# Two-branch attention layer: order of input-projection panels changed, sums of weights formed on VectorE

## Chip, cores and metric

One core of a Trainium2 chip runs the kernel. The metric is the device time of one execution in microseconds.

## The reference

One decoder layer on x of 1024 tokens x 2048 channels, all in float32, with a conditioning vector c of 2048:

```
shift, scale, gate = split(c @ w_ada + b_ada, 3)            # each 2048
h    = layer_norm(x) * (1 + scale) + shift
proj = h @ w_in       # 3 x 1024 (fox q,k,v), 8 forget logits, 1024 + 256 + 256 (swa q,k,v),
                      # 1024 + 1024 (g_fox, g_swa), 2048 + 2048 (m_fox, m_swa)
o_fox = forgetting_attention(8 heads of 128, causal, bias = differences of cumsum(log_sigmoid(logits)))
o_swa = sliding_window_attention(16 query heads of 64, 4 key/value heads, window 128, ALiBi, sinks)
y_fox = (o_fox * silu(g_fox)) @ w_br_fox ;  y_swa = (o_swa * silu(g_swa)) @ w_br_swa
merged = sigmoid(m_fox) * y_fox + sigmoid(m_swa) * y_swa
out  = layer_norm(2**0.25 * x + gate * (merged @ w_out)) * ln_g + ln_b
```

## The kernel before

Each engine has its own instruction stream, written out by hand, and they meet at semaphores. DMAs are issued by SyncE (SP), and some by GpSimd and ScalarE.

**Prologue.** Eight row blocks of x (128 x 2048) are loaded into a ring of four, their statistics taken (x_stat, x_scale on VectorE, x_norm on ScalarE) and transposed on TensorE. The part of shift and scale that the first half of the channels needs (c @ w_ada) is formed in four rounds: ada_sum on VectorE for half of the weights, ada_multiply on TensorE for the other half, ada_turn, ada_take. Loads for a round go out when its slots of the previous round are used.

**Input projection.** The output has 84 blocks of 128 channels (queries, keys and values of both branches: 36; gates g: 16; m: 32), and is formed transposed, as channels x tokens. The inner dimension is split into two panels of 1024. A group is two blocks in one panel, and is formed by a scheme of Strassen's kind with seven products in place of eight: `dense(q, lo, hi)` issues matmuls lo to hi of group q, `product(q, k)` being 12 of them (4 slices x 3 float32r parts: high x high, high x low, low x high), each 128x128 by 128x512. The factors on the weights' side are three blocks of the weights themselves and four sums or differences of blocks (`weight_sums`, on GpSimd at L580, into w_sum). Each factor is rounded to its high part on ScalarE (`weight_high`, L726) and its low part is formed on VectorE (`weight_low`, L1049). The factors of the activations' side, b_hi and b_lo, stay in SBUF for all groups of a panel. Weights of group q + 1 are loaded (`load_in`, L414, 1024 KB) once the last low part of group q that reads w_raw is formed. Products go through the PSUM banks pC, pA, pD, pC, pA, pC, pA; ScalarE takes the first use of a tile of ctile (`take`, L740), VectorE adds the others (`join`, L1056). After product k both engines do a fixed list of work in `after(q, k)`, waiting for the product first; ScalarE's list for k = 2 has the high part of the first factor of group q + 1, so it waits there for the load.

**Order.** GROUPS is 42. Groups 0 to 41 are panel one of all blocks; their results are stored to proj_scratch by SP (L433). Then panel two's operands replace panel one's in b_hi and b_lo (`renew`), and groups 42 to 83 are panel two, added to proj_scratch by DMAs with accumulation that GpSimd issues (L624): 10 groups (PRE) alone, 16 beside local attention, one in each unit (Q_SWA on), 16 beside forgetting attention, two in each head (Q_FOX on). FOX_AT tells after how many matmuls of a head's groups each row block's transposes stand, FOX_AFTER which steps `after` come in the row block.

**Conditioning of the rest.** The other half of shift and scale, and gate, are formed in four parts on VectorE, two bg_steps (L1081) in each of groups 0 to 31, from 2 x 512 KB a group that SP loads. Then bg_sum on TensorE adds over partitions.

**Attention.** A local unit is a block of 128 queries and 8 heads, handled in two halves e: scores(e), bias and maximum on VectorE, exponentials on ScalarE, normalising of two heads on GpSimd (L659) and two on VectorE, turn_weights(e) on TensorE, high and low parts, weigh(e). A head of forgetting attention goes over 8 row blocks i: scores(i), maximum, exponential, normalising on GpSimd (L678), turn_weights(i), high and low parts, and weigh of two row blocks together. Between these TensorE has matmuls of `dense`, so that it has work while the others handle the scores.

Then come the branch products (yP), the output product (zP), and the last norm, which the change does not touch.

## Time and profile before

| | us |
|---|---|
| median of 3 runs | 3051.3 |
| lowest, highest | 3049.14, 3057.31 |
| profiled execution, its own time | 3048.7 |
| its span, first to last instruction | 3047.0 |
| TensorE (PE) busy | 2746.3 |
| VectorE (DVE) busy | 1832.6 |
| ScalarE (ACT) busy | 1135.0 |
| GpSimd (POOL) busy | 890.8 |

The rows below are of one execution. Times are microseconds from the start of the span unless marked ns. PE is TensorE, PEld its weight loads, DVE VectorE, ACT ScalarE, POOL GpSimd, and SPq or POOLq a queue's own instructions. L1465 is a line of the kernel. A matmul's duration includes its pipeline, so 0.39 us for one that starts 0.23 after the last is no contradiction. `<-` in brackets names what ended an engine's idle time, and the number before it is how long that time was. In rows of stretches the order is: from and to, length, then busy us and instructions of PE, PEld, DVE, ACT and POOL, TensorE's granted clock as a share of its full one, the busy share of the 16 DMA engines, and GB/s.

### The profile page before, as it was taken

Reading aid. Unit: us, or ns where it says so; the run is one execution under the profiler, and the core shown is the slowest. Engines: PE = TensorE matmul, PEld = TensorE weight load, DVE = VectorE, ACT = ScalarE, POOL = GpSimd, SP = SyncE. Lnnn points to the kernel's source line nnn. Section 1 sums busy time; section 2 is a strip of 40 time slices with the busy share of each in tenths; the row PEclk is TensorE's granted clock in tenths of the full one; section 3 lists DMA queues with packets and bytes.
Section 4 is the critical chain, followed back from the end, with each engine's and each line's share of the span. In section 5 each row is a group of like instructions: output and inputs, shape, how many; then the busy total and the mean of one; then the engine's idle time right before and its main releaser. Section 6 shows DMA issues by size and latency. Waiting matters only on the chain. (4 is left out here: it accounts for less than half of the span.)

```text
span 3047.0 us, 39809 instructions
## 1 busy us (share of the span) xinstructions
PE 2746.3 (90%) x12241; PEld 2207.9 (72%) x12241; DVE 1832.6 (60%) x2433; ACT 1135.0 (37%) x2081; POOL 890.8 (29%) x693
## 2 busy tenths in 40 slices
PE   4799999999999899989889888988868999999895
PEld 3277777767788777777777777777756888888684
DVE  5565665656665785777878555555546446644335
ACT  5333233323233433455545434443434332344111
POOL 1333332323343444333433333333332000014002
PEclk7899999999999999999999999999988999999997
DMA  5534444334433245444344433344354445556442
GB/s 202 172 125 164 144 145 165 131 128 155 152 110 110 83 104 108 106 111 109 94 121 96 106 85 83 91 98 98 85 153 127 145 162 179 168 159 192 138 141 100
DMA packets 299057, 391.84 MB, mean 129 GB/s; under 512 B 15809, under 2 KB 226817, under 8 KB 297985
## 3 DMA queue, kind: packets, MB, share of 16 engines
q1 hardware_dynamic: 269472, 324.15, 32.6%
q0 software_dynamic: 16480, 58.75, 9.9%
q10 hardware_dynamic: 13056, 8.39, 0.9%
q8 instruction: 19, 0.31, 0.0%
q14 instruction: 30, 0.24, 0.0%
HBM read 286.37 MB, written 104.87 MB: 128 GB/s over the span
## 5 line engine op out<-in xcount | busy, mean ns | idle before, releaser
L1049 DVE TENSOR_TENSOR w_lo<-w_sum,w_hi 128x512 fp32r<-128x512 f32 x336 | 398.5, 1197 | 221.0 <-ACT w_hi L726 220.7
L580 POOL TENSOR_TENSOR w_sum<-w_raw 128x512 f32<-128x512 f32 x168 | 252.1, 1500 | 782.8 <-DMA w_raw<-in_w_in_dram 728.0
L1465 PE MATMUL pC<-b_hi,w_hi 128*128 128x512 f32 x1008 | 405.9, 403 | 47.3 <-DVE ctile L1056 35.9
L1465 PE MATMUL pA<-b_hi,w_hi 128*128 128x512 f32 x1008 | 395.7, 393 | 8.1 <-issue 5.3
L1465 PE MATMUL pC<-b_hi,w_lo 128*128 128x512 f32 x1008 | 400.6, 397 | 0.0
L1465 PE MATMUL pC<-b_lo,w_hi 128*128 128x512 f32 x1008 | 399.3, 396 | 0.0
L1465 PE MATMUL pA<-b_hi,w_lo 128*128 128x512 f32 x1008 | 397.8, 395 | 0.0
L1465 PE MATMUL pA<-b_lo,w_hi 128*128 128x512 f32 x1008 | 396.9, 394 | 0.0
L142 ACT CAST w_hi<-w_raw 128x1024 fp32r<-128x1024 f32 x128 | 134.9, 1054 | 422.1 <-PE zP L2127 208.0
L1056 DVE TENSOR_TENSOR ctile<-pA,ctile 128x512 f32<-128x512 f32 x252 | 165.8, 685 | 203.6 <-PE pA L1465 189.1
L147 DVE TENSOR_TENSOR w_lo<-w_raw,w_hi 128x1024 fp32r<-128x1024 f32 x128 | 159.6, 1247 | 193.6 <-ACT w_hi L142 192.6
L726 ACT CAST w_hi<-w_raw 128x512 fp32r<-128x512 f32 x252 | 156.9, 623 | 304.0 <-PE pA L1465 132.8
L1049 DVE TENSOR_TENSOR w_lo<-w_raw,w_hi 128x512 fp32r<-128x512 f32 x252 | 229.5, 911 | 63.3 <-ACT w_hi L726 63.2
L1465 PEld LDWEIGHTS pC<-b_hi,w_hi 128*128 128x128 f32 x1008 | 193.1, 192 | 102.1 <-DVE ctile L1056 47.8
L726 ACT CAST w_hi<-w_sum 128x512 fp32r<-128x512 f32 x336 | 209.2, 623 | 107.9 <-PE pA L1465 89.3
L2084 PE MATMUL yP<-og_hi,w_hi 128*128 128x512 f32 x512 | 203.3, 397 | 34.0 <-DVE og_lo L1923 31.5
L1465 PEld LDWEIGHTS pA<-b_hi,w_hi 128*128 128x128 f32 x1008 | 190.5, 189 | 49.6 <-issue 8.2
L1465 PEld LDWEIGHTS pC<-b_hi,w_lo 128*128 128x128 f32 x1008 | 194.2, 193 | 40.6
L1465 PEld LDWEIGHTS pC<-b_lo,w_hi 128*128 128x128 f32 x1008 | 193.1, 192 | 38.8
L1465 PEld LDWEIGHTS pA<-b_hi,w_lo 128*128 128x128 f32 x1008 | 191.2, 190 | 38.8
L1465 PEld LDWEIGHTS pA<-b_lo,w_hi 128*128 128x128 f32 x1008 | 191.2, 190 | 38.0
L2127 PE MATMUL zP<-w_hi,mg_hi 128*128 128x512 f32 x512 | 200.0, 391 | 12.2 <-DVE w_lo L147 12.2
(252 smaller groups left out, 5240.3 us busy)
## 6 DMA issues: line engine op xcount, KB each, us to landing
w_raw<-in_w_in_dram SPq DMA_DIRECT2D x84, 1024.0 KB, 7.9
proj_scratch<-ctile SPq DMA_DIRECT2D x84, 512.0 KB, 2.8
proj_scratch<-ctile POOLq DMA_DIRECT2D x84, 512.0 KB, 6.5
bg_raw<-in_w_ada_dram SPq DMA_DIRECT2D x64, 512.0 KB, 4.6
w_raw<-in_w_out_dram SPq DMA_DIRECT2D x64, 512.0 KB, 3.9
w_raw<-in_w_br_swa_dram SPq DMA_DIRECT2D x32, 512.0 KB, 4.0
w_raw<-in_w_br_fox_dram SPq DMA_DIRECT2D x32, 512.0 KB, 3.9
aux<-proj_scratch SPq DMA_DIRECT2D x64, 256.0 KB, 4.0
```

The costliest lines, as they stand in the source:

```text
L142: nc.scalar.copy(w_hi[:, slot, :], w_raw[:, slot, :]).then_inc(chunk_hi, 1)
L147: nc.vector.tensor_tensor(w_lo[:, slot, :], w_raw[:, slot, :], w_hi[:, slot, :].bitcast(F32), ALU.subtract).then_inc(chunk_lo, 1)
L580: nc.gpsimd.tensor_tensor(dst, a, b, op).then_inc(in_sums, 1)
L726: nc.scalar.copy(ring(k, False), factor(k)).then_inc(in_hi, 1)
L1049: nc.vector.tensor_tensor(ring(k, True), factor(k), ring(k, False).bitcast(F32), ALU.subtract).then_inc(in_lo, 1)
L1056: nc.vector.tensor_tensor(tiles[n], bank[:], tiles[n], ALU.add).then_inc(signal, 1)
L1465: last = nc.tensor.matmul(BANKS[k][:], w[:, j, :], b[:, j, :], start=(k < 4 and n == 0), stop=(n == 11), skip_group_check=True)
L2084: last = nc.tensor.matmul(yP[:, 2 * bank + br, :], w[:, slot, k * P:(k + 1) * P], o[:, 8 * br + k, :], start=(k == 0 and part == 0), stop= ...
L2127: last = nc.tensor.matmul(zP[:, tb, :], m[:, 2 * kk + k2, tb * P:(tb + 1) * P], w[:, kk % 2, k2 * HALF:(k2 + 1) * HALF], start=(kk == 0 an ...
```

## The change

The order of the projection becomes: panel one of queries, keys and values (groups 0 to 17), panel two of the same (18 to 35, added by GpSimd's DMAs), then panel two of the 24 gate groups beside local attention (36 to 59, three for each pair of units, stored by SP), and panel one of the gate groups beside forgetting attention (60 to 83, three for each head, added by GpSimd's DMAs). Panel one's operands are therefore saved to a DRAM scratch b_d (14 pieces of 1024 KB) during groups 1 to 7 and loaded back during the last group of local attention, each pair as soon as its product is done. `weight_sums` moves from GpSimd to VectorE, into `after` behind k = 2 and k = 4. The bg_steps stand behind k = 0 and 3 instead of 2 and 4, and their last two parts run in groups 19 to 34. GpSimd forms the four sums of panel two's activations all at the change of operands. In the prologue statistics of x run two blocks ahead of the scaling, and ada_sum one round further ahead. FOX_AT and FOX_AFTER are laid out anew, and SWA_AT and SWA_AFTER are added.

The diff, cut to its core:

```diff
-PRE = 10
-Q_SWA = GROUPS + PRE
-Q_FOX = Q_SWA + 16
+QKV = B_G // 2
+FOX_IN = B_SQ // 2
+Q_SWA = 2 * QKV
+Q_FOX = QKV + GROUPS
 BG_COLS = (D // 2, D + D // 2, 2 * D, 2 * D + D // 2)
 DVE_COLS = 1408
-FOX_AT = (16, 22, 30, 42, 58, 78, 102, 128, 156)
-FOX_AFTER = ((), (1,), (2,), (3,), (4, 5), (6, 7), (8, 9), (10, 11, 12))
+FOX_AT = (24, 41, 60, 82, 107, 136, 167, 201, 236)
+FOX_AFTER = ((2,), (3, 4), (5,), (6, 7), (8, 9, 10), (11, 12), (13, 14, 15), (16, 17, 18))
 TURNS = (0, 1, 2, 3, 4, 6, 8, 10)
+SWA_AT = (8, 58, 72, 108, 126)
+SWA_AFTER = ((0, 1, 4, 5, 6, 9, 9, 10), (10, 11, 15, 15, 16, 19, 20, 21))
...
+    b_d = nc.dram_tensor("b_scratch", (14, P, 4 * HALF), F32).ap()
...
+                def save(n):
+                    for low, buf in enumerate((b_hi, b_lo)):
+                        sp.dma_start(b_d[ds(n + 7 * low, 1), :, :].rearrange("a p t -> p (a t)"),
+                                     buf[:, ds(n, 1), :, :].rearrange("p a j t -> p (a j t)").bitcast(F32)).then_inc(b_saved, 16)
...
+                sp.wait_ge(b1_lo, 19)
                 with sp.Fori(1, 8) as q:
+                    save(q - 1)
                     group_in(q, True, 0)
...
+                with sp.Fori(16, 20) as n:
+                    load_bg(n, 2)
+                    load_in(n + (QKV - 14), column(n - 2, False), 1)
+                for n0, n1, part in ((20, 24, 2), (24, 32, 3)):
+                    with sp.Fori(n0, n1) as n:
+                        load_bg(n, part)
+                        load_in(n + (QKV - 14), column(n - 20, True), 1)
...
+                def unit_pair(g, m, last=False):
+                    u = 2 * m + 8 * g
+                    q = 3 * m + (Q_SWA + 12 * g)
+                    load_in(q + 1, column(q + (1 - QKV), False), 1)
+                    sp.wait_ge(s_prep, 2 * u + 3)
...
+                    store(q, 0, q - QKV)
+                    store(q, 1, q - QKV)
+                    load_in(q + 2, column(q + (2 - QKV), False), 1)
...
+                        load_in(q + 3, column(QKV, False), 0)
+                        sp.wait_ge(b_saved, 16 * 14)
+                        for k in range(7):
+                            sp.wait_ge(product_done, 7 * (q + 2) + k + 1)
+                            if k >= 2:
+                                sp.wait_ge(b3_loaded[k % 2], 32 * (k // 2))
+                            if k == 6:
+                                store(q + 2, 0, q + (2 - QKV))
+                            for buf, n in ((b_hi, k), (b_lo, LO_SLOT[k])):
+                                sp.dma_start(buf[:, n].rearrange("p j t -> p (j t)").bitcast(F32),
+                                             b_d[n + (7 if buf is b_lo else 0), :, :]).then_inc(b3_loaded[k % 2], 16)
+                    if not last:
+                        store(q + 2, 0, q + (2 - QKV))
+                    store(q + 2, 1, q + (2 - QKV))
...
+                        if i == 7:
+                            load_in(q + 2, column(q + (2 - GROUPS), False), 0)
...
+                pool.wait_ge(bg_added, 34)
+                nc.gpsimd.tensor_tensor(t1_raw[:], h_raw[:, 2], h_raw[:, 0], ALU.subtract).then_inc(b2_sums, 1)
+                pool.wait_ge(b2_sums, 1)
+                nc.gpsimd.tensor_tensor(h_raw[:, 2], h_raw[:, 3], h_raw[:, 2], ALU.subtract).then_inc(b2_sums, 1)
+                pool.wait_ge(b2_sums, 2)
+                pool.wait_ge(b2_lo, 2)
+                nc.gpsimd.tensor_tensor(h_raw[:, 0], h_raw[:, 2], h_raw[:, 0], ALU.add).then_inc(b2_sums, 1)
+                pool.wait_ge(b2_sums, 3)
+                pool.wait_ge(product_done, 7 * (QKV - 1) + 3)
+                nc.gpsimd.tensor_tensor(b_raw[:, 6], h_raw[:, 1], h_raw[:, 0], ALU.subtract).then_inc(b2_sums, 1)
...
+                        if phase[0] == 0:
+                            if not (isinstance(q, int) and q == 0):
                                 act.wait_ge(stored[row], 16 * q)
-                        elif p2[0]:
+                        elif phase[0] == 1:
+                            act.wait_ge(added[row], 16 * q - 16 * QKV)
+                        elif phase[0] == 2:
+                            act.wait_ge(stored[row], 16 * q - 16 * QKV)
+                        else:
                             act.wait_ge(added[row], 16 * q - 16 * GROUPS)
-                        else:
-                            act.wait_ge(stored[row], 16 * q)
...
+                def weight_sums(q, which):
+                    dve.wait_ge(in_loaded, 16 * q + 16)
+                    for n in which:
+                        if n in (1, 2):
+                            dve.wait_ge(in_sums, 4 * q + n)
+                        a, b, op = ((in_block(1, 0), in_block(1, 1), ALU.add),
+                                    (factor(3), in_block(0, 0), ALU.subtract),
+                                    (in_block(0, 1), factor(4), ALU.subtract),
+                                    (in_block(0, 0), in_block(1, 0), ALU.subtract))[n]
+                        dst = w_sum[:, n, :].rearrange("p (j n) -> p j n", j=4)
+                        nc.vector.tensor_tensor(dst, a, b, op).then_inc(in_sums, 1)
...
+                            weight_sums(q + 1, (0, 1))
...
+                    if k == 4 and more:
+                        weight_sums(q + 1, (2, 3))
...
-                def group(q, part=None):
+                def group(q, part=None, pair=None):
                     for k in range(7):
                         after(q, k)
-                        if part is not None and k in (2, 4):
-                            bg_step(q, k // 2 - 1, part)
+                        if part is not None and k in (0, 3):
+                            bg_step(q if pair is None else pair, k // 3, part)
...
+                x_stat(1)
                 for t in range(8):
-                    if t < 7:
-                        x_stat(t + 1)
+                    if t < 6:
+                        x_stat(t + 2)
                     x_scale(t)
-                for k in (0, 3, 4, 1, 2):
-                    weight_low(0, k)
                 dve.wait_ge(c_loaded, 32)
...
+                ada_sum(1)
+                ada_take(0)
+                weight_sums(0, range(4))
                 for p in range(4):
-                    ada_take(p)
+                    if p < 2:
+                        ada_sum(p + 2)
+                    b_low(p)
+                    if p == 0:
+                        for k in (0, 3, 4, 1, 2):
+                            weight_low(0, k)
                     if p < 3:
-                        ada_sum(p + 1)
-                    b_low(p)
...
+                            if isinstance(q, int) and q == Q_FOX:
+                                pe.wait_ge(b3_loaded[k % 2], 32 * (k // 2 + 1))
...
+                dense(16, 0, 84)
+                forget(4)
+                dense(17, 0, 84)
+                dense(QKV, 0, 84)
+                with pe.Fori(QKV + 1, 27) as q:
                     dense(q, 0, 84)
                 bg_sum(2)
-                forget(4)
-                with pe.Fori(24, 32) as q:
+                with pe.Fori(27, 35) as q:
                     dense(q, 0, 84)
                 bg_sum(3)
-                with pe.Fori(32, GROUPS) as q:
-                    dense(q, 0, 84)
-                dense(GROUPS, 0, 84)
-                with pe.Fori(GROUPS + 1, Q_SWA) as q:
-                    dense(q, 0, 84)
+                dense(35, 0, 84)
...
+                            at = [126 * par + n for n in SWA_AT]
+                            dense(q, 126 * par, at[0])
                             scores(0)
-                            dense(q, 2, 38)
+                            dense(q, at[0], at[1])
                             turn_weights(0)
                             scores(1)
-                            dense(q, 38, 48)
+                            dense(q, at[1], at[2])
                             weigh(0)
-                            dense(q, 48, 74)
+                            dense(q, at[2], at[3])
                             turn_weights(1)
-                            dense(q, 74, 84)
+                            dense(q, at[3], at[4])
...
-                    dense(q, FOX_AT[8], 168)
+                    dense(q, FOX_AT[8], 252)
```

## Rows read from the trace of the kernel before

**Rows 1.** Stretches of the span: us, busy by engine (instructions), TensorE clock, DMA share, GB/s.

```profile
0.00:134.30 134.30, 77.55 (x258) 36.45 (x258) 73.30 (x152) 53.92 (x77) 25.76 (x30) 0.81 0.58 196
...
134.30:1232.30 1098.00, 1040.63 (x4448) 833.40 (x4449) 692.82 (x684) 365.62 (x598) 387.86 (x246) 0.99 0.40 130
...
1232.30:1697.40 465.10, 416.95 (x2002) 341.85 (x2001) 361.62 (x610) 242.66 (x608) 168.57 (x160) 0.97 0.45 107
...
1697.40:2259.30 561.90, 503.01 (x2465) 415.66 (x2463) 313.65 (x526) 231.29 (x516) 190.43 (x157) 0.96 0.37 88
...
2259.30:3047.00 787.70, 708.14 (x3073) 580.55 (x3072) 391.17 (x462) 241.54 (x283) 118.19 (x100) 0.95 0.49 157
```

**Rows 2.** Chain that ended last: start, us, what.

```profile
2477.16 174.08 PE zP L2127 x768
```

**Rows 3.** Timeline, TensorE, start of a head: start, us, instruction.

```profile
1912.46 1.05 PE L1376 MATMUL tP<-ident,fv_raw 128*128 128x128 f32 x8
```

**Rows 4.** Waits of TensorE, 160 to 900 us: us, times, longest.

```profile
PE pC L1465 <- DVE ctile L1056: 35.9, 25, 2.3
```

**Rows 5.** Timeline, TensorE, first matmuls of two groups, [idle before <- by].

```profile
565.24 0.50 PE L1465 MATMUL pC<-b_hi,w_hi 128*128 128x512 f32 x1 [0.35 <-DVE ctile L1056]
...
585.91 0.50 PE L1465 MATMUL pC<-b_hi,w_hi 128*128 128x512 f32 x1 [1.34 <-DVE ctile L1056]
```

**Rows 6.** Timeline, VectorE, one group.

```profile
571.71 0.68 DVE L1049 TENSOR_TENSOR w_lo<-w_sum,w_hi 128x512 fp32r<-128x512 f32 x1
...
577.18 1.25 DVE L1049 TENSOR_TENSOR w_lo<-w_raw,w_hi 128x512 fp32r<-128x512 f32 x1 [1.62 <-ACT w_hi L726]
...
578.35 2.31 DVE L1081 SCALAR_TENSOR_TENSOR bg_acc<-bg_raw,c_sb,bg_acc 128x1024 f32<-128x1024 f32 x1
...
580.58 3.48 DVE L1049 TENSOR_TENSOR w_lo<-w_sum,w_hi 128x512 fp32r<-128x512 f32 x2
...
583.99 1.27 DVE L1081 SCALAR_TENSOR_TENSOR bg_acc<-bg_raw,c_sb,bg_acc 128x1024 f32<-128x1024 f32 x1
...
585.18 0.68 DVE L1056 TENSOR_TENSOR ctile<-pC,ctile 128x512 f32<-128x512 f32 x1
```

**Rows 7.** Timeline, GpSimd, same group.

```profile
581.77 1.74 POOL L580 TENSOR_TENSOR w_sum<-w_raw 128x512 f32<-128x512 f32 x1
```

**Rows 8.** Groups of instructions by line: count, busy us, mean ns, idle before.

```profile
L1049 DVE TENSOR_TENSOR w_lo<-w_sum,w_hi 128x512 fp32r<-128x512 f32 x336 | 398.5, 1197 | 221.0 <-ACT w_hi L726 220.7
...
L1056 DVE TENSOR_TENSOR ctile<-pA,ctile 128x512 f32<-128x512 f32 x252 | 165.8, 685 | 203.6 <-PE pA L1465 189.1 <-ACT ctile L740 13.5
```

**Rows 9.** Timeline, TensorE, transposes of weights, local unit and head.

```profile
1392.72 1.09 PE L1376 MATMUL tP<-ident,sp_w 128*128 128x128 f32 x8 [2.77 <-POOL sp_w L659]
...
1922.68 0.32 PE L1376 MATMUL tP<-ident,fp_w 128*128 128x128 f32 x1 [2.03 <-POOL fp_w L678]
```

**Rows 10.** Line 414, loads of weights, 1060 to 1232 us.

```profile
DMA to landing us min/median/max: 8.6/9.9/10.9
```

**Rows 11.** Line 414, 830 to 1000 us.

```profile
DMA to landing us min/median/max: 5.2/5.4/5.6
```

**Rows 12.** Line 414, 165 to 830 us.

```profile
DMA to landing us min/median/max: 5.7/7.2/8.1
```

**Rows 13.** DMA issues: count, KB each, median us to landing.

```profile
proj_scratch<-ctile SPq DMA_DIRECT2D x84, 512.0 KB, 2.8
...
fq_raw<-proj_scratch SPq DMA_DIRECT2D x64, 64.0 KB, 2.0
```

**Rows 14.** Timeline, VectorE, statistics of the fifth row block of x.

```profile
28.94 2.47 DVE L985 BATCH_NORM_STATS2 bn<-x_t 128x6 f32<-128x512 f32 x4 [3.04 <-DMA x_t<-in_x_dram]
```

**Rows 15.** Timeline, SyncE's queue, first load of x.

```profile
0.87 0.38 SPq L408 DMA_DIRECT2D x_t<-in_x_dram  x1
```

**Rows 16.** Timeline, TensorE, waits for ada loads.

```profile
83.02 5.71 PE L1404 MATMUL pC<-ada_ring,c_sb 128*1 128x512 f32 x8 [6.09 <-DMA ada_ring<-in_w_ada_dram]
...
118.11 5.24 PE L1404 MATMUL pC<-ada_ring,c_sb 128*1 128x512 f32 x8 [6.98 <-DMA ada_ring<-in_w_ada_dram]
```

420 lines of the change are left out of this document (209 added, 211 removed).

## The prediction

> **What bounds the kernel now.** I read the stretches first [rows 1]. TensorE works 90% of the span and its granted clock is 0.95 or more after the first 134.3 us, so the question is where its remaining time goes. A price for a product comes from the chain that ended last: 768 matmuls of 512 columns in 174.08 us [rows 2], 0.2267 us each. One product (12 matmuls) is then 2.72 us, and one group (seven products) 19.04 us. Against that price three stretches lose time. The 52 groups before local attention need 52 x 19.04 = 990 and take 1098: 108 lost. A unit of local attention holds one group and, by columns, 4096 for scores and 4096 for weighing (3.6 us) and 17 transposes at 1.05 / 8 = 0.13 us [rows 3] (2.2 us), so 24.8; 16 units need 398 and take 465.1: 67 lost. A head of forgetting attention holds two groups (38.1), 33280 columns (14.7) and 44 transposes (5.8), 58.6; eight need 469 and take 561.9: 93 lost. The last 787.7 us (branch products, output, norm) are not touched.
>
> Then I asked what ends those waits. Before the attention it is the bank pC, whose third tile VectorE joins late [rows 4]. Two neighbouring groups start at 565.24 and 585.91, so one lasts 20.67, 1.6 over the price, in each of the 32 groups that also carry a share of the conditioning sum (bg_step) [rows 5]. VectorE shows why: 0.68 us for a low part while GpSimd is idle, and two in 3.48 us while GpSimd forms sums of weights; the bg_step before them takes 2.31 against 1.27 after GpSimd is done; the join of pC then begins at 585.18, when TensorE has already run out [rows 6, 7]. Over the whole run a low part from w_sum averages 1197 ns, a join, which reads PSUM, 685 [rows 8]. In attention the waits are for normalised weights from GpSimd: 2.77 us in a local unit, 2.03 in the first row block of a head [rows 9], each where too few matmuls stand between scores and transposes.
>
> A rule of the Trainium skill (SBUF — State Buffer, Who interferes with whom) is that a VectorE instruction with two SBUF inputs contends with a GpSimd instruction that reads SBUF, one blocking the other for its whole length. The 3.48 against 0.68 agrees, and so does the join's steady 685. By that rule the low parts fall to their lone price once GpSimd is silent; by the run's mean taken as it stands they would not, which is rival (d). The rule also speaks against the change: the moved sums still collide in attention with GpSimd's normalising. If each of 32 local chains and 64 row blocks lost one sum's 0.6 us to that, the sum below would be 58 us higher; I take it as hidden by the larger filler.
>
> **The sums on VectorE.** 336 sums leave GpSimd and are added to VectorE. No row shows one there. Nearest is the low part from w_sum, same shape and two SBUF inputs: 0.68 long when alone, of which 0.6 to the next start (583.99 + 1.27 is 0.08 past 585.18) [rows 6]; the upper bound is 1.74, half of 3.48. With GpSimd silent I take 0.6. A group then costs VectorE 4 joins + 7 low parts + 4 sums = 15 x 0.6 = 9.0, and 2 bg_steps x 1.2 = 2.4: 11.4, against 692.8 / 52 = 13.3 now [rows 1]. What matters is the order after the next weights land. They landed 11.3 after the group's start (the first low part is at 11.9 after, 0.6 behind ScalarE's copy); the load is released by the last low part, now 0.5 earlier, so 10.8. From landing: ScalarE 0.5, low part 0.6, two sums 1.2, low part 0.6, bg_step 1.2, low part 0.6, two sums 1.2, join 0.6: 6.5, so pC is free at 17.3, before 19.04. The other limit is product 5 at 13.6, for which ScalarE must copy and take a tile after landing (1.2): weights may land at 12.4. So panel one's bg groups cost 19.04 but for about 0.1, and the 1.6 is gone.
>
> **Panel two of all blocks before attention.** Now 36 groups, not 52, stand before it. Groups 18 to 35 add to DRAM through GpSimd's queue. Beside such adds weights take 9.9 us to land, without 5.4 [rows 10, 11]. Released at 1.9, weights land at 11.8, inside 12.4, and pC is free at 18.3. The bg loads, which now run in 16 of these groups, cost a load behind them 7.2 - 5.4 = 1.8 [rows 11, 12]. They are issued earlier in the group than the weights, so I take 0.55 a group (10 us for 18), bounds 0 and 1.4 x 16 = 22.
>
> **Operands saved.** Groups 1 to 7 each put two stores of 1024 KB on SP's queue ahead of both bg loads, the weights and both result stores. A 512 KB store lands in 2.8 us and a 64 KB load in 2.0 [rows 13], so at best 0.8 per 512 KB, 3.2 in all; the nine 1024 KB pieces up to the fifth row block of x landed by 28.94 from 0.87 [rows 14, 15], 3.1 each, 6.2 in all. I take 4.5: landing 10.8 + 4.5 = 15.3, 2.9 past the limit of 12.4, x 7 = 20 us; bounds 1.6 x 7 = 11 and 4.6 x 7 = 32.
>
> **Operands restored.** In the last group of local attention 14 loads of 1024 KB go out, a pair per finished product, and SP's next load, the values of head 0, stands behind them; behind it stand keys, queries and weights. TensorE waits for the values before it starts the head. From the end of product 0: 14 x 3.1 = 43.4, the group's two stores 3.1, values 1.6, completion 2.0: 50. TensorE has six products (16.3), of attention 16 transposes, four score pairs and two weighings (2.1 + 0.9 + 1.8 = 4.8), and a gap of 1: 22. The stall is 28 us, and it goes nowhere else, since ScalarE and VectorE wait too. Bounds: 1.6 per piece (the store) gives about 5; 3.4 (5.4 - 2.0) gives 32.
>
> **Attention with more filler.** Local attention takes 24 groups of panel two of the gates, three per pair of units, stored rather than added. Between scores(0) and its transposes stand 50 matmuls (11.3 us) instead of 36 (8.2). The wait of 2.77 behind 8.2 makes a chain of 11.0: just covered. In the second unit of a pair VectorE forms two sums inside the chain (1.2), so some wait stays. I leave 2.5 a pair and 3 at entry, where ScalarE waits for the last adds: 23 lost, bounds 8 and 67. Heads take three groups; filler after scores(0) goes from 6 matmuls to 17 (3.9 us) against a chain of 1.4 + 2.03 = 3.4. I leave 2 a head, 16, bounds 8 and 93.
>
> **Prologue.** The statistics of x run two row blocks ahead, but scaling waits for them: by the rows' durations x is done 4.5 us later. In return VectorE's first ada sum starts before the last transposes, so the second round of ada loads is issued some 14 us earlier by the same count, and TensorE's waits for it, 6.09 and 6.98 [rows 16], go. Followed round by round, the first product starts at 121.3 instead of 134.3: -13, bounds 0 (the delay of x cancels the gain) and -20.
>
> **The sum**, on the profiled span of 3047.0. To the first product 121.3. Before attention 36 x 19.04 = 685, plus group 0's late low parts 10, saves 20, panel one 2, panel two 10, the change of operands after group 17 with GpSimd's four sums 12, forget(4) with 16 matmuls 4, bg_sum 8, the cumulative sum of gates on VectorE 4, unassigned 4 (the last four, and the 12, are allowances that no single row gives; the old stretch had the like): 759. Local attention 24 x 19.04 = 457, 16 x 5.8 = 93, plus 23: 573. Stall 28. Heads 457 + 8 x 20.5 = 164, plus 16: 637. End 787.7. Together 2906. The profiled execution took 3048.7, 1.7 over its span, and the median is 2.6 above that: 2910. The measurement can hardly tell less than 0.3% (9 us) from no change.
>
> **Rivals.** (a) The filler doesn't help, since VectorE and ScalarE run in order and pass the waits on: loss 67 instead of 23 and 93 instead of 16 give 2910 + 121 = 3031. For it: VectorE is 78% busy in local attention. Against: the waits are few per unit and at the places that get more filler. (b) Saving and restoring are hidden: 2910 - 48 = 2862. Against: the queue serves in order [rows 14, 15]. (c) Loads, not compute, set panel two and attention: each of 42 groups there over by 1.4, 2910 + 59 = 2969. (d) The other side: VectorE's sums cost 1.74 and the low parts stay at 1.2, so from landing to join there are 0.5 + 3 x 1.2 + 4 x 1.74 + 1.8 + 0.6 = 13.5, a period of 24.3, 5.3 over in 32 groups = 170, and about 36 in local attention: 3116. With a common price p (bg_step counts two) the period is 10.8 + 1.1 + 9p; it costs the forecast gain, 141 us over 32 groups, at p = 1.28. Against: 0.68 alone [rows 6].
>
> **Chances.** Sum as worked, 2880 to 2945: 0.60. (a) and partial forms up to 3040: 0.12. (b), or waits smaller than left: 0.14. (c): 0.10. (d): 0.04. The range 2865 to 2975 leaves out most of (a), (d) and the edge of (b), 0.2 in all. Faster by over 0.3%: 0.94; within: 0.03; slower: 0.03.
>
> **What would show it.** Groups 8 to 15 at 19.1 to 19.3 us; w_lo from w_sum near 0.7 and the new sums near 0.7; groups 1 to 7 near 22; a wait of TensorE of 20 us or more ahead of head 0; few waits for sp_w and fp_w; heads near 80 us; the first product near 121. It goes wrong if sums average above 1 us, if the restore costs twice what I gave, or if loads land later than 13 us after a group's start.

## The result, and the profile after

The changed kernel takes 2981.36 us (median of 4, 2978.66 to 2987.52) against 3053.23 (4 runs, 3049.14 to 3057.31) of the kernel before: ratio 0.9767, 95% interval 0.9747 to 0.9788. It is faster, by half of what was forecast: 2910 with a range of 2865 to 2975, so the time lies 6 us above the range.

The profiled execution's span is 2980.0 against the 2906 of the sum, 74 too long. The stretches of the changed kernel, to be laid beside [rows 1] (same columns). Shown are the time to the first product, groups 1 to 7 (157 to 327 us), groups 8 to 15, the change of operands (480 to 546), the other groups before local attention, local attention, the restore, the heads, and the part that was not touched:

```profile
0.00:123.10 123.10, 72.44 (x257) 32.81 (x257) 71.18 (x156) 53.41 (x77) 19.64 (x26) 0.93 0.64 214
...
157.00:327.00 170.00, 147.21 (x608) 117.14 (x607) 83.81 (x121) 44.14 (x77) 0.00 (x0) 0.95 0.60 218
327.00:480.00 153.00, 153.00 (x683) 126.73 (x683) 95.10 (x137) 51.16 (x89) 0.00 (x0) 1.00 0.47 162
480.00:546.00 66.00, 56.13 (x208) 36.76 (x207) 40.34 (x34) 30.02 (x35) 18.93 (x4) 0.92 0.18 60
546.00:908.90 362.90, 349.67 (x1498) 280.39 (x1497) 247.16 (x335) 117.11 (x201) 35.40 (x46) 0.99 0.62 149
908.90:1511.50 602.60, 559.59 (x2673) 457.47 (x2671) 457.65 (x793) 287.71 (x696) 52.20 (x65) 1.00 0.39 120
1511.50:1535.50 24.00, 0.38 (x3) 0.03 (x1) 1.94 (x4) 0.72 (x2) 0.00 (x0) 0.60 1.01 419
1535.50:2192.30 656.80, 637.57 (x3136) 528.70 (x3136) 396.57 (x704) 278.34 (x604) 115.06 (x112) 1.00 0.43 100
2192.30:2980.00 787.70, 709.44 (x3072) 581.62 (x3072) 390.68 (x461) 241.19 (x282) 116.97 (x100) 0.95 0.49 157
```

From 327 to 480 us TensorE is busy for 153.00 of 153.00: with the sums on VectorE eight groups in a row run at the price of their matmuls. So this step of the prediction is right. What fails is around it. In the 170 us ahead of that, where the copies are made, TensorE is busy for 147.

| stretch, us | forecast | measured | off by |
|---|---|---|---|
| to the first product | 121.3 | 123.1 | +2 |
| before local attention | 759 | 785.8 | +27 |
| local attention | 573 | 602.6 | +30 |
| stall of the restore | 28 | 24.0 | -4 |
| heads | 637 | 656.8 | +20 |
| rest | 787.7 | 787.7 | 0 |

The groups of instructions by line, beside [rows 8], with the new sums below (mean ns behind the busy time):

```profile
L1105 DVE TENSOR_TENSOR w_lo<-w_sum,w_hi 128x512 fp32r<-128x512 f32 x336 | 254.5, 762 | 175.9 <-ACT w_hi L758 173.9
...
L1112 DVE TENSOR_TENSOR ctile<-pA,ctile 128x512 f32<-128x512 f32 x252 | 165.8, 685 | 107.1 <-PE pA L1542 78.2
...
L1100 DVE TENSOR_TENSOR w_sum<-w_raw 128x512 f32<-128x512 f32 x168 | 119.1, 709 | 0.0
```

The low parts fell from 1197 to 762 ns and a sum costs 709, as forecast; rival (d) is out. The waits of TensorE in the two stretches with attention (us, times, longest; first local attention from 915 to 1500 us, then the heads from 1540 to 2190):

```profile
PE pC L1542 <- DVE ctile L1112: 16.2, 16, 1.5
PE pA L1542 <- DVE ctile L1112: 11.1, 9, 1.4
PE pA L1542 <- ACT ctile L774: 10.6, 8, 1.5
PE tP L1452 <- POOL sp_w L703: 2.1, 1, 2.1
...
PE pA L1542 <- ACT ctile L774: 7.1, 8, 1.1
PE oP L1700 <- DVE fpT L1405: 5.4, 8, 0.7
PE tP L1452 <- POOL fp_w L715: 4.7, 7, 1.6
```

In local attention the wait for normalised weights, which [rows 9] showed and which came to 44.8 us there, is 2.1. In its place stand 38 us of waits for banks: in this program TensorE writes pA or pC again only after ScalarE has copied and VectorE has joined the product that is in it.

Waits are not all that a stretch takes above the price of its matmuls. In local attention TensorE is idle for 43.0 us of 602.6 and busy for 559.6, with 550 priced. In the heads it is idle for 19.2 of 656.8 and busy for 637.6, with 621 priced.

### The profile page after: what moved, and what is told of

Its sections match the earlier page's. It is cut to its first block and busy times, and to the rows that moved or that the text cites. A ratio compares the mean times of both kernels' runs of the same rounds, so it can differ in the third digit from the quotient of the medians.

```text
span 2980.0 us, 39132 instructions
## 1 busy us (share of the span) xinstructions
PE 2716.4 (91%) x12241; PEld 2183.8 (73%) x12241; DVE 1806.2 (61%) x2769; ACT 1120.8 (38%) x2081; POOL 363.3 (12%) x357
## 5 line engine op out<-in xcount | busy, mean ns | idle before, releaser
L1105 DVE TENSOR_TENSOR w_lo<-w_sum,w_hi 128x512 fp32r<-128x512 f32 x336 | 254.5, 762 | 175.9 <-ACT w_hi L758 173.9
L1105 DVE TENSOR_TENSOR w_lo<-w_raw,w_hi 128x512 fp32r<-128x512 f32 x252 | 180.5, 717 | 49.3 <-ACT w_hi L758 49.3
L2166 PE MATMUL yP<-og_lo,w_hi 128*128 128x512 f32 x512 | 201.9, 394 | 0.0
```

Of the source, the lines that this page charges most:

```text
L1105: nc.vector.tensor_tensor(ring(k, True), factor(k), ring(k, False).bitcast(F32), ALU.subtract).then_inc(in_lo, 1)
L2166: last = nc.tensor.matmul(yP[:, 2 * bank + br, :], w[:, slot, k * P:(k + 1) * P], o[:, 8 * br + k, :], start=(k == 0 and part == 0), stop= ...
```

## The experiments

All lengths below are in us and read from one profile each, between the first matmuls of the third product (bank pD) of two groups, which is easy to find in a timeline. "Gap" is the two groups across the restore. The last column is the median of the timed runs, or a single run (s). Three of these kernels leave out work, as their texts say, and are there to price it: no copies, brief sums, plain transfers for adds.

| kernel | groups 1-7 | 8-15 | 16-18 | 19-35 | 36-58, local | gap | 61-82, heads | time |
|---|---|---|---|---|---|---|---|---|
| changed kernel | 169.4 | 154.3 | 83.5 | 352.5 | 577.7 | 75.2 | 599.7 | 2981.4 |
| copies late | 138.0 | 154.3 | 84.0 | 353.5 | 576.1 | 75.6 | 601.1 | 2949.0 |
| no copies | 135.1 | 154.1 | 83.7 | 352.6 | 577.2 | 58.0 | 599.1 | 2929.7 |
| brief sums | 169.0 | 154.1 | 83.3 | 355.4 | 559.3 | 73.3 | 582.5 | 2946.4 |
| order of local attention | 169.1 | 154.5 | 83.6 | 355.1 | 536.4 | 75.8 | 599.1 | 2941.3 |
| operand sums in pieces | 169.2 | 154.1 | 83.4 | 352.2 | 576.1 | 74.4 | 600.3 | 2978.3 s |
| operand sums on VectorE | 169.4 | 154.2 | 74.7 | 350.9 | 577.9 | 75.2 | 602.0 | 2972.3 s |
| plain transfers for adds | 169.2 | 154.1 | 83.7 | 338.9 | 575.4 | 74.4 | 603.0 | 2968.7 s |
| head 0 early | 169.1 | 154.1 | 83.6 | 352.9 | 577.6 | 74.8 | 601.9 | 2980.4 s |
| head 0 and stores early | 169.0 | 154.1 | 83.7 | 355.6 | 577.5 | 71.5 | 601.4 | 2978.5 s |
| sums behind turned weights | 169.4 | 154.1 | 83.7 | 356.2 | 575.9 | 73.3 | 596.1 | 2978.5 |
| four edits | 136.0 | 154.4 | 83.4 | 348.0 | 538.0 | 74.7 | 600.8 | 2908.6 |
| three edits | 136.0 | 154.1 | 83.2 | 355.4 | 536.9 | 71.2 | 601.5 | 2903.8 |
| five edits | 136.1 | 154.4 | 74.7 | 354.2 | 537.7 | 71.7 | 600.9 | 2892.2 |

Stretches that an edit does not touch repeat within 4 us (19-35 within some 8, the gap within 1.5), and a difference between two profiles tells nothing below that.

**Copies late.** Groups 1 to 7 take 24.2 us where 8 to 15 take 19.3. In one of them (timeline; idle time before an instruction and what ended it in brackets) VectorE waits for a load of conditioning weights (bg_raw) that SyncE issued behind the copy, and the join behind it on VectorE's list holds TensorE:

```profile
235.25 1.28 DVE L1140 SCALAR_TENSOR_TENSOR bg_acc<-bg_raw,c_sb,bg_acc 128x1024 f32<-128x1024 f32 x1 [9.95 <-DMA bg_raw<-in_w_ada_dram]
236.45 0.68 DVE L1112 TENSOR_TENSOR ctile<-pA,ctile 128x512 f32<-128x512 f32 x1
...
237.19 0.79 PE L1542 MATMUL pA<-b_hi,w_hi 128*128 128x512 f32 x1 [3.03 <-DVE ctile L1112]
237.78 0.63 PE L1542 MATMUL pA<-b_lo,w_hi 128*128 128x512 f32 x1
238.21 0.63 PE L1542 MATMUL pA<-b_hi,w_lo 128*128 128x512 f32 x1
```

Behind this wait the matmuls start 0.43 us apart instead of 0.23. From 237 to 243 us the granted clock is 0.50, the lower of its levels.

```diff
                 with sp.Fori(1, 8) as q:
-                    save(q - 1)
-                    group_in(q, True, 0)
+                    group_in(q, True, 0, kept=True)
...
                     load_in(q + 1, column(q + 1, fox), 0)
+                    if kept:
+                        save(q - 1)
                     store(q, 0, q)
```

> The changed kernel with each copy of an operand to device memory issued behind the loads of its group (row of the gate weight, next w_in slice) instead of ahead of them, in groups 1 to 7. Position theory: the copy costs only because the loads stand behind it on SyncE's queue, so groups 1 to 7 fall from about 24.0 us a group to the 19.1 of groups 8 to 15, some 33 us in all, and the time to about 2948. Traffic theory: the 2 MB of each copy share the DMA engines with the w_in load wherever they are issued, so the groups stay above 23 and the time within 7 us of 2981.

Measured: 2949.01 (ratio to before 0.9658, 0.9640 to 0.9675). Groups 1 to 7 take 138.0 and the weights land in 8.0 us instead of 9.7. The copy costs by its place: behind the loads it costs 2.9 of its 34.3 us. VectorE's waits for bg_raw in these groups (us, times, longest; the changed kernel from 157 to 327 us first, then the late copies from 157 to 295) fell by 33.5 us, about what the groups gained:

```profile
DVE bg_acc L1140 <- DMA bg_raw<-in_w_ada_dram: 69.6, 7, 10.0
```

```profile
DVE bg_acc L1141 <- DMA bg_raw<-in_w_ada_dram: 36.1, 7, 5.8
```

**No copies.**

```diff
-                    save(q - 1)
...
-                            for buf, n in ((b_hi, k), (b_lo, LO_SLOT[k])):
-                                sp.dma_start(buf[:, n].rearrange("p j t -> p (j t)").bitcast(F32),
-                                             b_d[n + (7 if buf is b_lo else 0), :, :]).then_inc(b3_loaded[k % 2], 16)
```

> The changed kernel without the copies of the panel-one operands to device memory and without their return; it leaves out that the last 24 groups multiply by the panel-one operands (they use those of panel two). Theory: groups 1 to 7 fall to 19.1 each (33 us) and the stall of 24 us ahead of the heads falls to 1 or 2, so the time is about 2925, and nothing changes in panel two, in local attention or in the heads. Rival: with the copies gone the groups 1 to 7 stay above 21 because the sums of weights on VectorE, not the copies, hold the next slice back; then the time stays above 2940.

Measured: 2929.72 (0.9601, 0.9582 to 0.9619). Saving costs 34.3 us in groups 1 to 7. About a third of that is not idle time: over these groups TensorE was idle for 22.8 us and busy for 146.6 at a mean clock of 0.95 in the changed kernel, and busy for all of 135.1 at 1.00 here. The return costs 17.2 net, since without it head 0 still waits 6 us for its values, where the theory had 1 or 2:

```profile
1483.42 0.90 PE L1441 MATMUL tP<-ident,fv_raw 128*128 128x128 f32 x3 [5.99 <-DMA fv_raw<-proj_scratch]
```

**The sums alone, on the kernel before.**

```diff
-                    weight_sums(q + 1, range(4))           # on GpSimd, in all its places
...
                             weight_low(q + 1, 0)
+                            weight_sums(q + 1, (0, 1))     # on VectorE, behind k = 2
...
+                    if k == 4 and more:
+                        weight_sums(q + 1, (2, 3))
```

> The kernel before with only the sums of weights moved from GpSimd to VectorE, at the places they have in the changed kernel; order of panels, groups and attention unchanged. Theory: 33 of the 36 groups ahead of local attention run near 19.1 us instead of 20.7 and more, some 50 us, and local attention, whose groups waited 44.8 us for GpSimd's shares of the weights, gains a part: 2960 to 3005. Rival: the sums are a load that the kernel before hides, and the gain of the changed kernel is all from spreading the groups over the two attention phases: then the time stays within 10 us of 3053.

Measured: 3031.63 (0.9929, 0.9911 to 0.9947), between the theory's range and the rival's. The theory had the sign, not the size. Groups 1 to 51, ahead of attention, fell from 1074.1 to 1035.3; 15 groups of local attention rose from 432.3 to 471.0; 15 groups of the heads fell by 12.9. TensorE's waits in local attention, first before, then with the sums on VectorE:

```profile
PE tP L1376 <- POOL sp_w L659: 44.8, 17, 3.3
```

```profile
PE tP L1355 <- POOL sp_w L633: 48.9, 28, 3.2
PE oP L1539 <- DVE spT_lo L1250: 11.2, 15, 0.8
PE pA L1444 <- ACT ctile L705: 3.9, 7, 0.8
```

Between the same two groups of local attention TensorE's idle time rose from 42.4 to 64.5 us, and its busy time for the same 1876 matmuls from 390.0 to 406.5, the granted clock falling from 0.97 to 0.96; that is the 39 us. Behind a wait of 2.75 us at 1425.22 its next 512-column matmuls start 0.43 apart. So moving the sums pays before attention and costs in it. That the sums now stand in VectorE's queue ahead of a unit's normalising and low parts, with too few matmuls to cover them, fits the waits but was not tested. Nor was the other half of the change alone, the new order with the sums on GpSimd: how much of the gain the order gives by itself stays open.

**Brief sums.**

```diff
+                        if brief[0]:
+                            dst, a, b = dst[:, :, 0:4], a[:, :, 0:4], b[:, :, 0:4]
                         nc.vector.tensor_tensor(dst, a, b, op).then_inc(in_sums, 1)
```

> The changed kernel in which, from local attention on to the end of the last product, the sums of weights on VectorE cover 4 columns of each of their four slices instead of 128; it leaves out the rest of these sums. That takes about 0.6 us from each of 192 VectorE operations, some 120 us of VectorE's time. Order theory: the attention phases lose their time to waits between in-order queues (a join behind a normalisation, a copy of a bank behind exponentials), so local attention falls from 602.6 by less than 12 us and the heads from 657 by less than 10. Load theory: VectorE's added work is what makes joins late, so local attention falls to 560 to 575 and the heads to 630 to 640.

Measured: 2946.36 (0.9649, 0.9630 to 0.9667). Local attention became 18 us shorter and the heads 17. In the heads' 22 groups TensorE's idle time fell from 16.5 us to 4.0. That is more than the order theory allowed in both. The load theory asked for 28 or more in local attention and didn't get it, and for 17 or more in the heads and did; so the two stages were looked at apart.

**Order of local attention.** Four times in a pair of units TensorE waits for a bank, three times for 1.3 to 1.5 us and once for 0.5. Two of these, one for VectorE and one for ScalarE (timeline):

```profile
1238.53 0.68 DVE L1349 TENSOR_TENSOR so_st<-oP,so_st 64x512 f32<-64x512 f32 x1
...
1239.53 1.18 DVE L1337 TENSOR_TENSOR sp_w<-sp_w,row_inv 128x256 f32<-128x256 f32 x2
1240.63 1.27 DVE L1112 TENSOR_TENSOR ctile<-pA,ctile 128x512 f32<-128x512 f32 x2
...
1257.45 0.51 ACT L906 ACTIVATE sp_w<-sp_w,neg_max 128x256 f32<-128x256 f32 x1 [2.19 <-DVE sink_exp L1326]
...
1259.54 0.56 ACT L774 COPY ctile<-pA 128x512 f32<-128x512 f32 x1
...
1242.06 0.47 PE L1542 MATMUL pA<-b_hi,w_hi 128*128 128x512 f32 x1 [1.32 <-DVE ctile L1112]
```

The last matmul of the two joins' product ended at 1238.0, and the joins start 2.6 us later: a low part, a half's output and a normalisation come first in the list. The last row is TensorE's wait for them. ScalarE's copy of pA stands behind four exponentials, ahead of which ScalarE was idle for 2.19 us.

```diff
-SWA_AFTER = ((0, 1, 4, 5, 6, 9, 9, 10), (10, 11, 15, 15, 16, 19, 20, 21))
+SWA_AFTER = ((0, 1, 4, 5, 7, 9, 9, 10), (10, 12, 15, 15, 16, 19, 20, 21))
```

> The changed kernel with two places of the fixed order of local attention moved: the joins of the seventh product stand ahead of the second normalisation of an even unit, and ScalarE's copy of the twelfth product's bank ahead of the first exponentials of an odd unit (VectorE's next join moves with it). No work is added or removed. Order theory: of the 5.8 us that a pair of units takes above its matmuls, the shorter sums of weights took back 2 and the rest is waits behind such neighbours, so a pair falls from 74.5 to 70 to 73 and the time by 12 to 35 us. Load theory: VectorE and ScalarE are late as a whole, the wait shows up behind the next instruction, and the pair stays within 0.7 us of 74.5 or grows.

Measured: 2941.31 (0.9638, 0.9613 to 0.9662), 40 us below the changed kernel and more than the order theory's 12 to 35. A pair fell from 74.5 to 69.6 us, beside 68.7 of matmuls, with every sum at full size. The waits of 915 to 1470 us:

```profile
PE pC L1542 <- DVE ctile L1112: 4.4, 8, 0.8
PE tP L1452 <- POOL sp_w L703: 2.1, 1, 2.1
PE pA L1542 <- DVE ctile L1112: 0.3, 1, 0.3
```

So in local attention the order decides: with all of VectorE's work kept, 41 of the 51 us that groups 36 to 58 took above the price of their matmuls (577.7 for 526.8) are gone. Brief sums, with 18, only shortened what stood ahead of the joins. Which of the two moved places gives how much was not tried.

**Sums behind the turned weights, in the heads.** The same question there. `half_out` and `turned_low` stand behind the list of `after`; four pairs of sums per head are moved behind them.

```diff
                         for n in FOX_AFTER[i]:
-                            after(q + n // 7, n % 7, not (last and n >= 14))
+                            after(q + n // 7, n % 7, not (last and n >= 14), hold=(n in (2, 4, 11, 18)))
...
                         turned_low(i)
+                        while held:
+                            weight_sums(*held.pop(0))
```

> The changed kernel with four pairs of sums of weights per head of the last phase moved on VectorE's queue from ahead of the low part of the turned weights to behind it. No work is added or removed. Order theory: in a head TensorE waits 0.69 us for that low part because two sums of 0.69 stand ahead of it, and the normalisation that follows is late in the same way, so a head falls from 81.5 to 79.5 to 80.8 us and the eight together give 6 to 16 us: 2965 to 2975. Load theory: VectorE's total is what counts, the wait moves to the next join, and the time stays within 4 us of 2981.

Measured: 2978.45 (0.9759, 0.9740 to 0.9777). That is 2.9 us below the changed kernel, inside the load theory's 4. The profile's heads are 3.6 us shorter over 22 groups, under the 6 of the order theory and no more than untouched stretches differ. The wait for fpT, 5.4 us, is gone, and the two others grew by 2.2 (heads, 1540 to 2150 us):

```profile
PE pA L1547 <- ACT ctile L774: 8.2, 7, 2.3
PE tP L1457 <- POOL fp_w L715: 5.8, 7, 0.9
```

Brief sums got 17 us in the same stretch. In the heads this order does not recover what the shorter sums did: the load theory's forecast came true here, and whether another order would do better was not tried.

**Operand sums in pieces.** After group 17 GpSimd forms four sums of 128x2048, and VectorE's operations with two SBUF inputs last as long as they do (timeline of the changed kernel; the last row is what TensorE waited):

```profile
521.87 2.28 DVE L1211 TENSOR_TENSOR b_lo<-h_raw,b_hi 128x2048 fp32r<-128x2048 f32 x1
...
524.30 4.87 POOL L649 TENSOR_TENSOR h_raw<-h_raw 128x2048 f32<-128x2048 f32 x1 [5.70 <-DVE b_lo L1211]
...
524.68 5.05 DVE L1105 TENSOR_TENSOR w_lo<-w_raw,w_hi 128x512 fp32r<-128x512 f32 x1
...
529.25 4.83 POOL L652 TENSOR_TENSOR b_raw<-h_raw 128x2048 f32<-128x2048 f32 x1
...
529.65 4.98 DVE L1100 TENSOR_TENSOR w_sum<-w_raw 128x512 f32<-128x512 f32 x1
...
535.90 0.76 PE L1542 MATMUL pA<-b_hi,w_hi 128*128 128x512 f32 x1 [8.68 <-ACT ctile L774]
```

The trace agrees with the Trainium skill (SBUF — State Buffer, Who interferes with whom) that such a VectorE instruction and a GpSimd instruction that reads SBUF contend: 5.0 us instead of 0.68, beside GpSimd's 4.8 to 4.9.

```diff
+                def in_pieces(dst, a, b, op):
+                    for p in range(4):
+                        last = nc.gpsimd.tensor_tensor(dst[:, p], a[:, p], b[:, p], op)
+                    last.then_inc(b2_sums, 1)
```

> The changed kernel with each of the four GpSimd sums that make the panel-two operands (128x2048 elements, 4.6 to 4.9 us each) cut into four of 128x512. Block theory: a two-input operation of VectorE that meets one of GpSimd waits for its whole length, so the 5 us rows of VectorE between 510 and 535 us become 1 to 2 us, and the two groups around the operand change (33.1 and 31.4 us) lose 5 to 10 us together. Rival: the groups wait for the sums themselves, whose total stays 19 us or grows by the fixed part of 12 more instructions; then the two groups change by less than 2 us or grow.

Measured: 2978.28, groups 16 to 18 unchanged (83.4), as the rival had it. VectorE's longest rows of 512 elements fell from 5.0 to 1.8 us. But more of its rows are held up, and GpSimd's pieces take 2 us each beside it, its four sums 28.0 us in all instead of 18.9:

```profile
512.26 1.29 POOL L644 TENSOR_TENSOR t_raw<-h_raw 128x512 f32<-128x512 f32 x1
513.62 16.34 POOL L644 TENSOR_TENSOR h_raw<-h_raw 128x512 f32<-128x512 f32 x8
```

**Operand sums on VectorE.**

```diff
+                operand_sum(0, t1_raw[:], h_raw[:, 2], h_raw[:, 0], ALU.subtract)
+                operand_sum(1, h_raw[:, 2], h_raw[:, 3], h_raw[:, 2], ALU.subtract)
                 for k in range(7):
                     after(QKV - 1, k)
...
+                    if k == 1:
+                        operand_sum(2, h_raw[:, 0], h_raw[:, 2], h_raw[:, 0], ALU.add)
+                    if k == 2:
+                        operand_sum(3, b_raw[:, 6], h_raw[:, 1], h_raw[:, 0], ALU.subtract)
```

> The changed kernel with the four sums that make the panel-two operands on VectorE, in the order of its queue, instead of on GpSimd. Block theory: GpSimd's four sums of 4.8 us held VectorE's two-input work for their length; on VectorE they are 4 times some 2.3 us, the 5 us rows go, and the two groups around the operand change (33.1 and 31.4 us) lose 4 to 10 us together. Rival: what those groups wait for is the serial chain of 28 conversions on ScalarE and VectorE, and adding 9 us to VectorE makes them longer.

Measured: 2972.27; groups 16 to 18 fell by 8.8, inside the block theory's 4 to 10. VectorE does 2048 elements a partition in 2.29 us, GpSimd in 4.6 to 4.9:

```profile
509.35 2.29 DVE L1205 TENSOR_TENSOR t_raw<-h_raw 128x2048 f32<-128x2048 f32 x1 [11.94 <-PE sP L1515]
```

**Plain transfers for adds.**

```diff
                     pool.dma_start(proj_d[ds(dst + row, 1), :, :].rearrange("a p t -> p (a t)"), ctile[:, row, :],
-                                   accum_op=ALU.add).then_inc(added[row], 16)
+                                   **kind).then_inc(added[row], 16)
```

> The changed kernel with the 18 panel-two groups ahead of local attention stored by plain transfers on GpSimd's queue instead of accumulating ones; it leaves out that panel two is added to panel one for these rows. Theory: ScalarE's 122 us of waits for the accumulating transfers (5.3 to 10.5 us to land) are what takes those groups from 19.1 to a mean of 20.5 us, so 546 to 909 us shortens by 15 to 25. Rival: w_in slices that land in 9.6 us where they had 8.1 are late by themselves, and the same stretch shortens by less than 5.

Measured: 2968.71. Groups 19 to 35 fell by 13.6, 1 short of the theory's 15 and above the rival's 5; the other runs lie between 348.0 and 356.2. The next slice of weights lands in 6.7 us where it took 9.6 beside the adds, so the adds slow their neighbours too, and the run changes both at once. ScalarE's own waits speak for the theory: from 546 to 909 us it waited 130.6 us for the adds and 12.2 for weights; here (546 to 895) 5.9 for the transfers and 3.8 for weights.

**Head 0 early, then its stores too.** The restore is where TensorE stands longest:

```profile
1535.48 0.90 PE L1452 MATMUL tP<-ident,fv_raw 128*128 128x128 f32 x3 [23.62 <-DMA fv_raw<-proj_scratch]
```

```diff
                             if k >= 2:
                                 sp.wait_ge(b3_loaded[k % 2], 32 * (k // 2))
+                            if k == 2:
+                                first_head_in()
```

> The changed kernel with the loads of values, keys and the first queries of head 0 issued between the second and third panel-one operands on their way back, instead of behind all seven. Queue theory: TensorE stood 23.6 us because the values are last on SyncE's queue, and the operands of the fifth to seventh products are not needed for another 25 us; the interval of the group across the gap falls from 49.3 to 32 to 37 and the time by 12 to 17 us. Rival: the same 15 MB have to land, and the first group of the head then stands for its operands: the gap moves by one group and the two intervals together (75.2) fall by less than 4.

Measured: 2980.41, the gap 74.8 instead of 75.2. TensorE turned the values 26 us earlier, at 1509.8, did two products, and stood for what was now last in the queue. ScalarE waited for the stores of local attention's last group, and TensorE behind it (idle time named "issue"):

```profile
1535.08 0.31 ACT L984 ACTIVATE fq_hi<-fq_raw 128x128 fp32r<-128x128 f32 x1 [24.51 <-DMA proj_scratch<-ctile]
...
1539.04 0.45 PE L1694 MATMUL sP<-cum_k,fcq 128*128 128x128 f32 x1 [22.73 <-issue]
```

So these stores went ahead as well:

```diff
-                            if k == 6:
+                            if k == 4:
                                 store(q + 2, 0, q + (2 - QKV))
+                                store(q + 2, 1, q + (2 - QKV))
```

> The changed kernel with head 0's values, keys and first queries loaded between the second and third returning operands, as in the run before it, and with the two stores of local attention's last group issued ahead of the fifth returning operand instead of behind the sixth and seventh. In the run with the early loads alone ScalarE stood 24.5 us for those stores, behind the operands on SyncE's queue, and that held head 0's copies and then TensorE 22.7 us. Theory: with the stores ahead as well the interval across the gap falls from 46.7 to 27 to 33 us and the time from 2980 to 2962 to 2970. Rival: the returning operands themselves are what is late, since the fifth to seventh still land at 1525 to 1537, and TensorE stands 10 us or more for them a product or two later.

Measured: 2978.47, the gap 71.5. It is now two waits, 8.5 and 9.4 us; the second goes back to ScalarE, which stood 15 us for the queries of the second row block:

```profile
1543.77 0.31 ACT L985 ACTIVATE fq_hi<-fq_raw 128x128 fp32r<-128x128 f32 x1 [14.99 <-DMA fq_raw<-proj_scratch]
```

Both queue theories failed, and the two rivals hold as far as the total goes. In the changed kernel some 19 MB move from 1488 to 1535.5 us (401 GB/s on the mean, 419 in the last 24 us, with all 16 DMA engines busy), and in both runs what was put ahead made something else last.

**Edits together.**

> The changed kernel with the late copies, the two moved places of local attention, the sums in pieces and the early loads of head 0 together. The four lie in different stages, so their effects add: 32 for the late copies, 12 to 35, 5 to 10 and 12 to 17 us. Theory: 2885 to 2920. Rival: what one stage gives is taken by the next, as a slice loaded earlier finds the engines late in turn; then the time is above 2930.

Measured: 2908.55 (0.9525, 0.9504 to 0.9546): copies late, order, pieces, head 0 early; inside the theory, though the last two give 4 us of the 17 or more that it asked of them and the order gives more than its share, and 72.8 us below the changed kernel where the single effects add to 76.

> The late copies, the two moved places of local attention, and head 0's loads with the two stores ahead, together; the operand sums stay whole on GpSimd. Against the kernel with four edits (2908.6) only the stores count: theory 2889 to 2898. Rival: the gap ahead of the heads stays at 20 us and the time at 2905 to 2910.

Measured: 2903.83 (0.9523, 0.9510 to 0.9536): above the theory's 2898 and 1 us under the rival's 2905; against head 0 early alone the stores give 3.5 us of the gap, as before.

> The late copies, the two moved places of local attention, head 0's loads and the last two stores ahead, the operand sums on VectorE, and the sums behind the turned weights in the heads. Against the kernel with the first three (2903.8) the operand sums count for 9 and the sums in the heads for 6 to 16: theory 2879 to 2890. Rival: gains in one stage are taken back in the next: above 2895.

Measured: 2892.21 (0.9471, 0.9458 to 0.9484), the fastest kernel of the study, 89 us below the changed one. It is between the theory's 2890 and the rival's 2895: the 9 us of the operand sums came as alone (8.5 in groups 16 to 18), the heads' order gave nothing that can be told.

## Why the prediction was right and wrong

**Right.** Sums near 0.7 us and low parts near 0.7 (measured 0.709 and 0.762); groups 8 to 15 at 19.3; the wait for sp_w gone; a stall of more than 20 us ahead of head 0, priced 28 and 24.0 (44.5 us from the first returning load to the first transpose for the 50 of the sum, since at 419 GB/s a piece takes 2.5 us and not 3.1); the first product at 123.1 for 121.3, with the two waits for ada loads, 13.1 us in the kernel before, gone; the change of operands itself (groups 16 to 18 hold 57.1 of groups and 13.9 of forget(4), which leaves 12.5 for the 12 of the sum). The last is luck: the 12 was an allowance from no row, and VectorE held up by GpSimd's sums, which makes 8.8 of it, was not in the working.

**Wrong, term by term.** The 74 us lie in these, the largest of them the order of the lists in local attention.

- *Saves, 20 for 34.3* (no copies against the changed kernel), just above the bound of 32. The step that failed is that the limit was the weights' landing. The copy delays the loads for bg_step as well, and with bg_step behind k = 0 the join of pA waits for it (VectorE's waits for bg_raw, 69.6 against 36.1 us). The sum also had no term for the clock, which was granted at 0.50 behind some of these waits. Placed behind the loads, the same bytes cost 2.9.
- *forget(4), 4 for 13.9.* It was priced as 16 matmuls at the 0.2267 of float32r operands. The program has 16, but the operands are float32, and the trace holds two records for each, 0.43 us apart: 0.87 a matmul. The trace of before has this row too (32 records from 649.4 to 662.7 us), and it was not looked up. It is in both kernels, so it cost the forecast 10 us and the change nothing. The row of the changed kernel:

```profile
495.31 13.90 PE L1511 MATMUL sP<-h_raw,flw 128*8 128x512 f32 x32
```

- *Panel two before attention, 10 for 17.* Groups 19 to 35 took 352.5 for 323.7 of matmuls; 4 for the cumulative sum, 4 for two bg_sums and 4 unassigned, which are the sum's own allowances and no measurements, leave 17. The 10 were for loads behind the gate weights'. What cost was the adds, of which the sum had only the landing of the weights (9.9 taken, 9.6 measured) and not ScalarE's takes, which wait for them: plain transfers took out 13.6.
- *Local attention, 23 over its matmuls for 53.* This is the largest miss. The failing sentence is "so some wait stays. I leave 2.5 a pair". It followed only the chain that was late before, the one for sp_w, and asked whether more filler covers it. It did. But a third group for each pair of units puts its copies and joins among the same lists too, and the banks became what is late. A pair takes 5.8 us above its matmuls, and 0.9 with two places of the order moved. Order alone gives back 41 of the stretch; the forecast is missed by 30.
- *Heads, 16 for 36.* Here the 2 a head that were left for waits are right: the waits listed above come to 17 us over eight heads. What failed is the step before, the price of a head's own matmuls, 457 + 8 x 20.5 = 621, where TensorE was busy for 637.6 at a mean clock of 1.00. The rows had it: [rows 1] give 503.0 busy us in the old heads, and the prediction priced them at 469 and took all 93 us above as waits, of which 58.9 were idle time. Part of the excess goes with the waits, but with brief sums, which leave 4.0 us idle in 22 groups, TensorE is still busy for 578.4 where the price is 569. Which matmuls take more than their price was not taken apart.

Rival (a), that in-order queues pass the waits on, had its mechanism in local attention, with 30 us of its 44 there; in the heads, where it asked for 77, the waits came as the sum had them. Rival (c), 1.4 a group in panel two and attention, has 1.0 a group in panel two, from the adds; in neither attention phase does a wait of TensorE name a load. Rival (b) was half true: saving can be hidden, restoring was not, in either order that was tried. Five terms were off to the same side, and the range gave that no room.

**Where the expected gain went.** Of 141 us forecast, 67 came in span. By losses against the price of the matmuls: before attention 108 became 100 (the copies, the adds and the change of operands now lie in fewer groups), local attention 67 became 53, the heads 93 became 36, the restore is 24 new, and the first product comes 11 earlier.

## What to carry to other kernels

When work is spread between the stages of an attention, follow not only the chain that was late but every shared bank: list what stands ahead of each copy and join in its engine's fixed order, since two numbers there were worth 40 us here. Before calling what a stretch takes above a price per matmul waits, take its idle time apart from its busy time; the rows of stretches give both. Put bulk transfers that nothing waits for behind the loads of their group on an in-order queue, and read what else stands behind them, not only the next weights. Where all DMA engines are busy, as in the restore, two reorderings gave 0.4 and 3.7 us of a gap of 75; there, count the bytes.

## What the runs showed of the hardware that was not expected

- Cutting GpSimd's sums into pieces shortens each block on VectorE (5.0 to 1.8 us) but not the stretch (83.5 and 83.4): the pieces of 1.29 us alone take 2.04 while VectorE works.
- The same sum of 2048 elements a partition takes VectorE 2.29 us and GpSimd 4.6 to 4.9.
- With one core at work the restore moved 419 GB/s, for 24 us with every DMA engine busy. The Trainium skill (Perfetto Trace Analysis, Roofline) gives a single core's 16 DMA engines about 435 GB/s together; the trace agrees.
- While TensorE stood for the restore its clock was granted at 0.50, the lower of its levels (from 1523 to 1535.5 us; 0.60 over the whole stall), and its first matmuls behind the stall start 0.43 us apart instead of 0.23.
- A matmul of 512 columns with 8 stationary columns and float32 operands stands in the trace as two records 0.43 us apart and takes 0.87 us (forget(4) above, 16 in 13.9 us), 3.8 times the 0.2267 of a float32r one.
